# The MLP's scales and gate are summed in other stages, the gate on GpSimd

## The reference

```python
def ada_modulation(cond, w, b):
    m = jax.nn.silu(cond) @ w + b
    return jnp.split(m[..., None, :], N_MOD, axis=-1)

sh_a, sc_a, g_a, sh_m, sc_m, g_m = ada_modulation(c, w_ada[layer], b_ada[layer])
csh_a, csc_a, cg_a, csh_m, csc_m, cg_m = ada_modulation(c_ctx, w_ada[layer], b_ada[layer])
...
x = x + g_a * (jnp.concatenate([attn, pool], axis=-1) @ w_out[layer])
hm = modulate(rms_norm_2(x, norm_mlp_w[layer]), sh_m, sc_m)
x = x + g_m * squared_relu_mlp(hm, w_mlp_up[layer], w_mlp_down[layer])
```

## Time and profile before

| | us |
|---|---|
| median of 3 runs | 1814.24 |
| lowest and highest run | 1813.35 to 1815.23 |
| the profiled execution: its time | 1812.95 |
| its span, first to last instruction | 1811.3 |

### The profile page before, as it was taken

One profiled execution on the slowest core, in us unless ns is written; L12 is line 12 of the kernel. 1 busy time (PEld: TensorE's weight loads), 2 busy tenths in 40 slices (PEclk: granted clock), 3 DMA queues, 4 the chain that ended last, 5 costly groups with the idle time before them and its releaser, 6 DMA issues.

```text
span 1811.3 us, 34903 instructions
## 1 busy us (share of the span) xinstructions
PE 1671.5 (92%) x12462; PEld 1508.9 (83%) x12462; DVE 1050.5 (58%) x1568; ACT 759.0 (42%) x1068; POOL 31.5 (2%) x48
## 2 busy tenths in 40 slices
PE   3899999899988986999889869999999999999996
PEld 2788888788877876878779859989998999899985
DVE  4445454455556557467665575655556555555675
ACT  5344444334333334344344434434443454345442
POOL 0000000000000000000000000000000000000000
PEclk9899999899998998999999969999999999999998
DMA  7677777688874775673225515555555555555552
GB/s 311 242 268 251 276 269 258 214 302 288 301 283 167 286 258 192 256 291 117 94 70 175 176 68 185 185 186 181 180 186 192 183 183 186 185 184 183 185 189 92
DMA packets 88370, 374.71 MB, mean 207 GB/s; under 512 B 10256, under 2 KB 10768, under 8 KB 75488
## 3 DMA queue, kind: packets, MB, share of 16 engines
q1 hardware_dynamic: 87120, 369.54, 59.0%
q0 software_dynamic: 1168, 4.00, 0.7%
HBM read 371.40 MB, written 2.10 MB: 206 GB/s over the span
## 4 chain that ended last, share of the span: by engine, by line
issue 72%; PE 16%; DVE 8%; ACT 3%; POOL 0%; DVEq 0%; ACTq 0%; POOLq 0%
PE G L400 4%; PE G L401 4%; PE G L402 4%; DVE lo L1050 3%; ACT hi L731 1%; PE ADA L441 1%; PE M L624 1%; PE S L611 1%; PE ADA L638 1%; PE S L598 1%; DVE t L1097 0%; DVE resid L1512 0%; DVE sm L1344 0%; DVE blk L1050 0%; PE S L599 0%
## 5 line engine op out<-in xcount | busy, mean ns | idle before, releaser
L1050 DVE TENSOR_TENSOR lo<-raw,hi 128x1024 fp32r<-128x1024 f32 x496 | 607.8, 1225 | 427.9 <-ACT hi L731 396.1
L400 PE MATMUL G<-actA,hi 128*128 128x256 f32 x2368 | 691.8, 292 | 31.7 <-DVE actA L1050 31.1
L731 ACT ACTIVATE hi<-raw 128x1024 fp32r<-128x1024 f32 x496 | 525.6, 1060 | 387.3 <-PE G L427 194.6
L401 PE MATMUL G<-actA,lo 128*128 128x256 f32 x2368 | 676.5, 286 | 0.0
L402 PE MATMUL G<-actA,hi 128*128 128x256 f32 x2368 | 676.2, 286 | 0.0
L400 PEld LDWEIGHTS G<-actA,hi 128*128 128x128 f32 x2368 | 458.6, 194 | 93.0 <-issue 73.9
L401 PEld LDWEIGHTS G<-actA,lo 128*128 128x128 f32 x2368 | 459.2, 194 | 0.4
L402 PEld LDWEIGHTS G<-actA,hi 128*128 128x128 f32 x2368 | 458.7, 194 | 0.0
L426 PE MATMUL G<-actB,hi 128*128 128x512 f32 x1024 | 358.6, 395 | 0.0
L427 PE MATMUL G<-actB,lo 128*128 128x256 f32 x1024 | 287.5, 281 | 0.0
L426 PEld LDWEIGHTS G<-actB,hi 128*128 128x128 f32 x1024 | 192.2, 188 | 44.5
(11 more groups left out here) (173 smaller groups left out, 1004.8 us busy)
## 6 DMA issues: line engine op xcount, KB each, us to landing
raw<-stream_dram SPq DMA_DIRECT2D x496, 512.0 KB, 4.2
ada_raw<-w_ada_dram SPq DMA_DIRECT2D x96, 1024.0 KB, 6.5
x_tok<-x_tok_dram SPq DMA_DIRECT2D x1, 2048.0 KB, 8.3
resid<-xT_dram SPq DMA_DIRECT2D x1, 2048.0 KB, 10.9
ctx_tok<-ctx_tok_dram SPq DMA_DIRECT2D x1, 2048.0 KB, 17.9
W<-ctxT_dram POOLq DMA_DIRECT2D x16, 128.0 KB, 6.1
out_dram<-resid SPq DMA_DIRECT2D x4, 512.0 KB, 2.6
ada_raw<-pool_w_dram POOLq DMA_DIRECT2D x1, 1024.0 KB, 6.9
```

The source lines that it names most:

```text
L400: pe.matmul(bank, hi[:, slot, cols], x[:, k, 0:T], start=(k == 0), stop=False, skip_group_check=True)
L401: pe.matmul(bank, lo[:, slot, cols], x[:, k, 0:T], start=False, stop=False, skip_group_check=True)
L731: return act.activation(dst, src, ACT.Copy)
L1050: return dve.tensor_tensor(dst, a, b, op)
```

## The change

- Block 4 (the scales) moves to where block 5 was, and starts earlier: one row before each of units 2, 3 and 4 of `U_KV`, one after each of units 4 to 6 as before, and one after unit 7; then four rows in each of query tiles 0 and 1 and one in tile 2. Its copy stands at the end of query tile 2, its turn in query tile 3.
- The first output stage sums no row. Only block 3's turn stays, in its first unit.
- Block 5 (the gate) is no longer summed by matmuls of the modulation. SP loads 1 MB at a time, cut another way (for one tile k of the input: 4 x 512 columns for each partition, 2 KB pieces), into `ada_raw`'s first buffer. GpSimd multiplies each 128 x 512 piece by `silu(c)`'s tile k into `adas` and adds it to a sum of 128 x 2048 (`gate_part`), and waits for each step's end. The loads stand in front of every fourth weight half of the down units of groups 0 and 1, 8 in each, and each waits until GpSimd has taken the whole load before it.
- Before the last group TensorE sums `gate_part` over the partitions with 16 matmuls against a column of ones, and VectorE adds the bias before the last down units.

```diff
+SCALE_LOADS = {U_KV + 2: 1, U_KV + 3: 1, U_KV + 4: 1, U_KV + 5: 1, U_KV + 6: 1, U_KV + 7: 2,
+               U_Q: 2, U_Q + 1: 2, U_Q + 2: 2, U_Q + 3: 1}
...
+        gate_part = W[:, 1024:3072]
+        gate_raw, gate_c = ada_raw[:, 0], cpad[:].rearrange("p k n -> p (k n)")
...
+            def gate_load(k):
+
+                m, g = divmod(k, 4)
+                src = ada_w[5 * KT:6 * KT].rearrange("(n m) p (g c) -> m g p n c", m=4, g=4)[m, g]
+                if k:
+                    sp.wait_ge(gate_taken, 4 * k)
+                sp.dma_start(gate_raw, src).then_inc(gate_full, 16)
+
+            at = U_OUT2
+            for g in range(2):
+                weights(at, U_MLP + 2 * KT * g + KT)
+                if g == 0:
+                    sp.wait_ge(pool_ready, 4)
+                for i in range(8):
+                    gate_load(8 * g + i)
+                    at = U_MLP + 2 * KT * g + KT + 2 * i
+                    for n in range(2 * at + 8, 2 * at + 12):
+                        weight(n % RING, n)
+                at += 2
+            weights(at, UNITS - 4)
...
-            pool.wait_ge(ada_used, 96)
+            pool.wait_ge(ada_used, 4 * KT + KT)
             pool.dma_start(pool_w, t_in["pool_w"]).then_inc(pool_in, 16)
+            pool.wait_ge(w_used, 2 * U_OUT2 + 2)
+            pool.memset(gate_part, 0.0).then_inc(gate_zero, 1)
             power(14)
             pool.memset(acc, 0.0).then_inc(acc_zero, 1)
+            pool.wait_ge(gate_zero, 1)
+            for k in range(KT):
+                pool.wait_ge(gate_full, 16 * (k + 1))
+                for m in range(4):
+                    part = gate_part[:, m * 512:(m + 1) * 512]
+                    pool.tensor_scalar(adas, gate_raw[:, m, :], cpad[:, k, 6:7], None, ALU.mult).then_inc(gate_scaled, 1)
+                    pool.wait_ge(gate_scaled, 4 * k + m + 1)
+                    pool.tensor_tensor(part, part, adas, ALU.add).then_inc(gate_taken, 1)
+                    pool.wait_ge(gate_taken, 4 * k + m + 1)
...
             for n in range(UNITS_OUT):
-                unit(At(U_OUT1), n, actB, inB, ada=U_OUT1 + n)
+                half_unit(At(U_OUT1), n, 0, actB, inB)
+                if n == 0:
+                    ada_turn()
+                half_unit(At(U_OUT1), n, 1, actB, inB)
...
-            half_unit(at, 0, 0, actC, inC)
-            ada_turn()
-            half_unit(at, 0, 1, actC, inC)
+            unit(at, 0, actC, inC)
             total_sums(1)
             half_unit(at, 1, 0, actC)
             broadcast()
             half_unit(at, 1, 1, actC)
+            ada_rows(4 * KT)
             unit(at, 2, actC)
+            ada_rows(4 * KT + 1)
             unit(at, 3, actC)
+            ada_rows(4 * KT + 2)
...
+            def gate_sums():
+
+                pe.wait_ge(gate_taken, 4 * KT)
+                for m in range(KT):
+                    x = pe.matmul(S[0][:, m:m + 1], gate_part[:, m * P:(m + 1) * P], ones[:, 0:1], start=(m == 0), stop=(m == KT - 1),
+                                  skip_group_check=True)
+                x.then_inc(gate_summed, 1)
```

More of the change, by code:

```diff
@@ L291, in _ @@
             ada(1, 1, first=True)
-            with sp.Fori(0, U_KV // 4 - 1) as i:
+            with sp.Fori(0, U_OUT1 // 4) as i:
                 for j in range(4):
@@ L296, in _, with weights @@
                     weight((2 * j + 1) % RING, i * 8 + 2 * j + 9)
[L297 to L303 removed]
+            with sp.Fori(0, UNITS_OUT // 4) as i:
+                for j in range(8):
+                    weight(j % RING, i * 8 + 2 * U_OUT1 + 8 + j)
             e = 2
             for u in range(U_KV, U_OUT2):
[L306 to L309 removed]
+                for _ in range(SCALE_LOADS.get(u, 0)):
+                    ada_load(4 * KT + e, e % 2, ada_used, 4 * KT + e - 1)
+                    e += 1
                 weight(2 * u % RING, 2 * u + 8)
                 weight((2 * u + 1) % RING, 2 * u + 9)
[L312 to L314 removed]
+            def weights(first, last):
+                with sp.Fori(0, 2 * (last - first) // RING) as i:
+                    for j in range(RING):
+                        weight(j, i * RING + 2 * first + 8 + j)
+            def gate_load(k):
[16 more added lines that the diff above has]
+            weights(at, UNITS - 4)
             for i in range(4):
@@ L1496, in _ @@
                 else:
+                    dve.wait_ge(gate_summed, 1)
+                    seq(tt(adav[:, 0, G_M:G_M + KT], S[0][:, 0:KT], col("b_ada", 5 * KT, KT), ALU.add))
                     with turn.lap(dve, 7, "dve last down") as i:
```

48 lines of the change are left out of this document (18 added, 30 removed).

## The result

The changed kernel takes 1998.97 us (median of four runs, 1998.65 to 1999.58) against 1814.38 us before: a ratio of 1.1019, with a 95% interval of 1.1002 to 1.1035. The direction was forecast, the size was not: 1855 was predicted, 1890 was the top of the range, and the gate alone was to cost 47 us. The profiled execution took 1999.03 us.

A forecast was written before the change was run, and what follows sets the result against it. TensorE was taken to bound the MLP, a circle of VectorE and ScalarE the first output stage. 1812.95 - 5.8 (-1.0 - 4.0 + 0 - 5.0 + 4.2) + 47 = 1854.2, with 1.3 for the median 1855 us; range 1807 to 1890.

The forecast's parts named there:

- step 6: Gate loads in SP's queue during down units: landing, GpSimd's work and sharing make a 16.4 us cycle, costing 47 us.
- Step 4: Queries: fewer rows in tile 2 and no late turn in tile 3 gain 5.0 us; bounds 3.0 and 5.5.
- Step 5: Before the last group: TensorE's 16 sums cost 4.2 us on its path; bounds 2.5 and 4.5.
- Step 1: First output stage: 16 rows leave, 17.1 us of TensorE's time, but gain only 1.0 us; bounds 0 and 17.1.
- the circle: First output stage: VectorE and ScalarE wait on each other, 7.66 us a unit, against 6.9 us that TensorE needs.
- Step 2: First key unit: moving the scales' turn out gains 4.0 us; bounds 3 and 4.3.
- Step 3: Keys and values: three added rows, 3.2 us, are covered by TensorE's idle times in the fifth unit; cost 0.
- free lead: Down units: weights are loaded four units ahead, so 12.9 us of delay in each group cost nothing.
- the forecast's own case: Gate in the down units: cycle of 15 to 17.3 us, time 1830 to 1866 us; chance 0.35.
- Hidden: Down units: GpSimd's part with waits under 8.2 us, so the lead covers the gate; 1808 us, chance 0.14.
- GpSimd slower but undisturbed: Down units: cycle 13.4 us without disturbance by VectorE; 1813 to 1836 us, say 1820; chance 0.18.
- Full exclusion: Down units: GpSimd and VectorE exclude each other, all four `lo` hold GpSimd up; cycle 18.3 us, time 1882; chance 0.25.

## Why the prediction was wrong, step by step

The forecast missed by 144 us. The gate's loads and arithmetic cost 183.5 us and not 47, which is 137 of them (step 6); the other 7 lie mostly in steps 4 and 5. The step that failed is the cycle of 16.4 us in step 6, in two of its terms, landing and GpSimd's own time.

**Step 1, right.** VectorE's waits in the first output stage of the changed kernel are the same as in the earlier trace rows:

```profile
DVE lo L1100 <- ACT hi L782: 35.4, 15, 2.5
```

The stage is 1.05 us shorter, 1.0 was forecast, though 17 us of TensorE's work had gone. The units ran at 5.8 us, where they had run at 6.9, until the circle caught them; that was at the sixth unit and not at the eleventh, and the later ones took 7.7 to 8.2.

**Step 2, right.** The wait for the first key unit's sums fell from 4.89 us to 1.20. The unit takes 14.2 instead of 17.9 us, and moving the turn alone brought 3.0 us in the whole kernel. There it stands behind the second unit, which is 1.6 us longer by it.

**Step 3, right.** Keys and values are 4.7 us shorter in all, where steps 2 and 3 made 4.0. The three rows lengthen the second to fourth units by 0.8 or 0.9 us each, and the fifth unit gives it back: 15.3 us instead of 18.5. No step had two small losses: the second output stage is 0.5 us longer and the first group's up units 1.1, with and without a gate; their cause is open.

**Step 4, wrong by 4.0 us.** The failed step is "3 x 1.0 + 2.3 = 5.3", taken from the distance of 23.4 us between the scores of tiles 2 and 3. Rows and a turn lay in that distance, but most of it was VectorE's: softmax, window sums, low parts. I compared it with 19.7 us of the next tile and put the difference down to the rows; what the next tile lacks is the window sums too. With the same rows gone the distance is 22.0 us in the kernel with the rows earlier, 1.4 less, and 23.7 in the changed kernel, where the granted clock fell ahead of the scores. Between tiles 1 and 2, with no such chain, one row fewer gave 0.9 us (22.1 to 21.2).

**Step 5, its term right, its consequences missing.** The sums take 3.5 us (4.2 forecast, 2.5 to 4.5):

```profile
1792.95 3.63 PE L757 MATMUL S<-ones,W 128*128 128x1 f32 x32
```

That a clock and a pace would follow was not in it; in the kernel without a gate it made 7.3 us.

**Step 6, the circle right, two of its three terms too small and the lead too large.** In us for each cycle:

| term | forecast | measured | from |
|---|---|---|---|
| landing | 4.8 | 9.6 | mean of 14 waits; 4.9 with whole rows |
| GpSimd undisturbed, with its waits | 8.6 | 12.0 | 4 x 3.01 |
| sharing with VectorE | 3.0 | 3.1 | 15.1 - 12.0 |
| sum c | 16.4 | 24.7 | loads of one group |
| free lead, each group | 12.9 | 2 | 7 x (24.7 - 11.3) - 91.7 |

*Landing.* The step that failed is "The pieces are shorter here; I keep 4.8". Cut into pieces of 2 KB a load of the same size took 4.3 to 4.6 us more. The earlier trace rows showed loads of long pieces alone, and I noted the difference without a bound for it. Whole rows took 4.6 us off each cycle, 64 in 14, and 75 off the kernel, with the weights behind them.

*GpSimd.* This is the second step that failed. The bounds of 5.1 to 10.2 came from memset rows, and the 12.0 measured lie over both: the multiply takes 1.56 us for 512 columns and not 0.96 at most, the add 1.26 against 1.38. No row stood behind the step from a memset to a multiply. For the add the Trainium skill's figure (GPSIMD Engine Reference, Elementwise and Engine selection) gave an estimate of 1.1 to 1.2 us, and the traces nearly agree, with 1.26. GpSimd's part was 3.4 us a cycle too small, 48 in all.

*Sharing.* 3.1 against 3.0, but the 3.0 was a choice between two bounds, so that it fits is luck. The mechanism is that of the rival: GpSimd waits for the rest of each `lo` that it meets. What the rival had too high is the price, 4 x 1.225 = 4.9 us, since an instruction that begins within a `lo` waits for what is left of it; the four waits of the cycle above were 0.7 to 0.9 us each. `lo` goes from 1.225 to 1.4 to 2.1 us, and with GpSimd's own queue up to 2.35. The Trainium skill (SBUF — State Buffer, Who interferes with whom) has whichever of the two begins first keep the shared port until its end while the other waits; the trace agrees within 0.14 us for GpSimd behind `lo` and `lo` behind an add, and shows less for `lo` behind a multiply. That GpSimd's reading is the condition for a two-input instruction, as it states there, agrees: beside 128 memsets no `lo` was over 1.3 us.

*Lead.* With the measured cycles, 7 x (c - 11.3) less the measured cost of a group leaves 2.1 us for the changed kernel, 2.1 with adds alone, 1.6 with memsets, and 7.5 with whole rows. Of the 10.8 us lost, 5.0 went to the weights behind a gate load, which landed 11.0 us after their issue and not 6.0. The clock took 1.9 to 2.7: the granted clock is 0.80 and 0.81 over the two down stretches, where the earlier trace rows has 1.00, and a slow unit between two stalls costs nothing, as the cycle covers it, but the one behind a group's last stall, the third up unit of the next group, takes 8.5 and 7.7 us where 5.8 is the rule. The first of the two:

```profile
1345.10:1353.60 8.50, 8.48 (x48) 8.48 (x49) 7.42 (x6) 4.41 (x6) 8.05 (x6) 0.65 0.60 186
```

The other 3 to 4 us are open.

By its own formula, with the measured cycle, 1.5 us for all the rest and the forecast lead, the prediction would have been 1812.95 + 1.3 + 1.5 + 2 x (7 x 13.4 - 12.9) = 1978; the last 21 us are the lead. (The same formula gives 1836 for c = 15 and not the 1830 with which the forecast's own case began.) "Hidden" and "GpSimd slower but undisturbed" are out, since c is 24.7 and sharing costs 3.1 of it. Full exclusion was right about who waits for whom, but its 1866 to 1895 us missed for the same two terms, landing and GpSimd's own time, as the forecast.

## What to carry to other kernels

A load that waits for a slow consumer does not belong in the queue that feeds the fast one: issued by GpSimd itself, in whole rows and once VectorE's norm work was over, the same gate cost 0.8 us, within the noise, instead of 183. Before a load is priced by its bytes, look at its pieces, and before an instruction is priced by another kind, look for a row of its own kind: here a multiply cost more than an add, and both more than a memset. And a work item that lies inside a distance is not the cause of the distance; look first for the engine that has no idle time in it.

## What the runs showed of the hardware

- Pieces of 2 KB: 1 MB landed in 9.2 us and not 4.9, and 2 MB of weights issued behind it in 11.0 and not 7.0.
- GpSimd's multiply of a tile by one number for each partition (one tile read, 1.56 us for 128x512) was slower than its add of two tiles (1.26).
- Where GpSimd read and VectorE ran a `lo` (two tiles read), the later of the two waited for the earlier, GpSimd always to within 0.14 us of the `lo`'s end.
- A memset of GpSimd never stretched `lo` (none of 496 over 1.23 us in either kernel with memsets), but it stretched VectorE's add of one number for each partition to one tile of 128x256 from 0.353 us to as much as 1.72.
- The down units run at one of two paces, 88.8 or 90.5 us for 16, at a full granted clock in both. In the kernel before, groups 0 and 2 have the slow one, groups 1 and 3 the fast one; TensorE's 16 sums turned group 3 to the slow one, and without them it went back. Group 3 is slow in all eleven kernels that have these sums and fast in all seven that have not. The sums are not the only thing that turns it: in the kernel with GpSimd's arithmetic alone group 1 is slow and group 2 fast. What sets it is open.
- In the kernel without a gate the 16 sums, with one column each, were followed by 3.4 us at 1.2 GHz, although TensorE's records show it busy all through; in the changed kernel's profiled execution they were not (its up units behind the sums take 92.2 us and not 93.7).
